# Up projections with the low and high part of x in one 512-column product, and the second layer's embedding product in four pieces elsewhere

## The chip, the cores and the metric

The kernel runs on one core of one Trainium2 chip. The metric is the device time of one execution in microseconds (us). A run's time is compared with runs of the kernel before; of the kernel before, three runs are given.

## The reference, cut to what matters

Two transformer blocks on one sequence of 256 tokens with 1024 features, all in float32. The first block has two layers. Each layer mixes tokens (layer 0 by two recurrences, layer 1 by attention), then has a feed-forward part and a gated embedding:

```
for l in range(2):
    x = x + mix(rms_norm(x, attn_norm[l]))
    h = rms_norm(x, mlp_norm[l])
    x = x + jnp.square(jax.nn.relu(h @ w_up[l])) @ w_down[l]      # 1024 -> 4096 -> 1024
    ple = rms_norm(p[l] @ ple_proj[l], ple_norm[l])               # 256 -> 1024
    x = x + ple * jax.nn.sigmoid(x @ ple_gate[l])
```

The second block follows with its own mixer and a mixture of 32 experts, of which all weights are read (some 200 MB).

## The kernel before, in words

Engines work through programs written out by hand, one per engine, each in order; they meet at semaphores. Weights come in units of 128 x 4096 floats (2 MB) through a ring of three slots; SP issues the loads in the order of a list of units, each when the unit three places earlier was read (L2836). The list of a layer's feed-forward part is: eight up units (512 of 4096 hidden features each), eight down units, one unit for the embedding's weights ("ple"), two gate units. Layer 1's ple stands between the last down unit and the gates.

Products of nearly full precision are made from rounded halves. A float32 weight w is split into high (w rounded to the matmul's short format, by ACT, `split_high` L2438) and low (w minus high, by DVE, `split_low` L1740, written over w in its ring slot); x likewise into `turned_high` and `turned_low` (ACT L2450, L2446; DVE L1755, L1750). A product then takes three passes, high x high, high x low and low x high (`three_passes`, L935), into the same columns of a PSUM bank. A unit is split in two halves; there are four buffers for high halves.

The up projection (`split_features`, `split_first`) holds weights still and streams x, 256 tokens: one half unit makes two blocks of 128 features, 256 columns each, in one bank of 512 columns. ACT evacuates a bank with ReLU (L2421) into one of four buffers `relu`; DVE squares it (L2077), rounds it (L2078) and takes the low part (L2079), which counts up `act_ready`. In each pass over a unit c, ACT first splits unit c + 1 (both halves), then evacuates the two banks of c; DVE does the same in its own order. The last pass splits the first down unit in place of an up unit.

`split_first` makes the first up unit in an order of its own, since the second half of x arrives late: half the features of two blocks, then a callback that turns the rest of x (transposes, L874), then what is left. Before the loop ACT also takes the norm's sums of squares and its square root (`norm`, L2426, L2427).

The down projection streams weights, 512 columns a product, 48 products a unit. After it x is turned again (`x_gate`), p is turned (L874), and for both layers the embedding product `p @ ple_proj` is made by `to_tokens` (L917: eight float32 products of 512 columns, two instructions each) while ACT and DVE make `turned_high` and `turned_low`; then come the gate products. POOL's queue loads p, the norms' rows and other small tables.

Attention's program for layer 1: six qkv units, transposes of q and k, the score and value products (`attend`), the output projection `w_o`. There are eight PSUM banks, taken in turn; PE waits before it takes one that was not read.

Of the kernel before, what the change touches and what calls it, by code (L numbers as in the profile page):

```python
# [7 lines left out]
P = 128  # L8
# [9 lines left out]
D = 1024  # L18
# [165 lines left out]
def weight_units(a):  # L184
# [55 lines left out]
def build(nc, a, out):  # L240
    ctx = ExitStack()
    with ctx:
# [140 lines left out]
        p_tok, pT = blocks(half(40), NT), blocks(half(41), 2)  # L383
        ple_raw, gate_s, ple_squares = (blocks(page(i, 2), NT) for i in (0, 2, 4))
# [125 lines left out]
        turned_high, turned_low = as_parts("turned_high", xn_at, KC * S), as_parts("turned_low", hT_at, KC * S)  # L510
# [358 lines left out]
        def _(pe):  # L869
# [67 lines left out]

            def split_features(name, tag, after=(None, None), first=False, turned_as=None):
# [28 lines left out]
            def split_first(name, tag, turned_as, between):  # L967

                pair = [banks.take(pe, *tag, s) for s in range(2)]

                def column(s, i, ks):
                    high, low_ = half_ready(name, s)
                    m = slice(i * P, (i + 1) * P)
                    for k in ks:
                        a = slice(k * S, (k + 1) * S)
                        if i == 0 and s == 0 and k % 2 == 0:
                            banks.wait_read(pe, *turned_as, k // 2)
                        last = three_passes(pair[s].ap[:, i * S:(i + 1) * S], high[:, k, m], low_[:, k, m],
                                            turned_high[:, a], turned_low[:, a], True, k == 0, k == KC - 1)
                    return last  # L980
# [6 lines left out]
                for s in range(2):  # L987
                    column(s, 1, range(KC)).then_inc(pair[s].full, 1)
                    half_read[(name, s)] = (pair[s].full, pair[s].use + 1)
                read_by(pair[1], *name)  # L990
# [382 lines left out]

            def feed_forward(l):
# [11 lines left out]
                split_first(("up", l, 0), ("up", l, 0), ("h_mlp", l), turn_late)  # L1386
                for c in range(1, 8):
                    split_features(("up", l, c), ("up", l, c))
# [9 lines left out]
                pe.wait_ge(sem("p_landed"), 16 * (l + 1))  # L1398
                bank = banks.take(pe, "pT", l)
                transposes([(bank.ap[:, k * S + t * P:k * S + (t + 1) * P], p_tok[:, t, k * P:(k + 1) * P])  # L1400
                            for k in range(2) for t in range(NT)], bank)
# [13 lines left out]
                banks.wait_read(pe, "pT", l)  # L1415
                w = blocks(weights(pe, "ple", l)[:, 0:2 * D], 2)
                for n in range(2):
                    bank = to_tokens(("ple", l, n), w[:, :, n * 512:(n + 1) * 512], pT, 2, 512)
                read_by(bank, "ple", l)
                def turn_early():  # L1420
                    pe.wait_ge(sem("ple_added"), NT)
                    turn_some(("h_att",), (0, 1))

# [40 lines left out]
            def turn_late():  # L1464
                pe.wait_ge(sem("ple_added"), 2 * NT)
                turn_some(("h_att",), (2, 3))

# [15 lines left out]
            turn_heads("kT", k_tok)  # L1483
            for tag in ("qT", "kT"):
                for c in range(4):
                    banks.wait_read(pe, tag, c)
            attend("att", lambda h: qT[:, h, :], lambda h: kT[:, h, :],
                   lambda h, k: v_att[:, k, h * P:(h + 1) * P], "att_prob", prob, probT)
            for c in range(4):
# [206 lines left out]
        def _(dve):  # L1696
# [366 lines left out]
            def feed_forward(l):  # L2063
                for c in range(8):
                    if c < 7:
                        split_low("up", l, c + 1)
                    else:
                        split_low("down", l, 0, 0)
                    if c == 0:
                        scales(2 if l == 0 else 4)  # L2070
                        step(v.tensor_tensor(rstd2, rstd, rstd, ALU.mult))
                    for i in range(2):
                        banks.wait_read(dve, "up", l, c, i)
                        buf = relu[:, (2 * c + i) % 4, :]
# [27 lines left out]
                for t in range(NT):  # L2102
                    step(v.scalar_tensor_tensor(ple_raw[:, t, :], ple_raw[:, t, :], ssq[:, t:t + 1], big_row,
                                                ALU.mult, ALU.mult))
                def add_gated(n):
                    for t in range(NT):
                        banks.wait_read(dve, "gate", l, n, t)
                        cols = slice(n * 512, (n + 1) * 512)
                        gated, part = ple_raw[:, t, cols], x3[:, t, cols]
# [91 lines left out]
            v.reciprocal(rstd, rstd).then_inc(sem("in2_scale"), 1)  # L2201
            dve.wait_ge(sem("in2_scale"), 1)
# [41 lines left out]
            v.reciprocal(cs, cs).then_inc(sem("latent_scale"), 1)  # L2244
            dve.wait_ge(sem("latent_scale"), 1)
# [90 lines left out]
            v.reciprocal(rstd, rstd).then_inc(sem("rstd_ready"), 1)  # L2336
            dve.wait_ge(sem("rstd_ready"), 1)
# [73 lines left out]
        def _(act):  # L2411
# [174 lines left out]

            def feed_forward(l):
                banks.read(act, "w_out" if l == 0 else "w_o", 0, 0)
                split_high("up", l, 0)
                take_highs(("h_mlp", l), range(KC // 2), lambda k: v1("mlp_norm", 8 * l + k))  # L2590
                for n in range(2):
# [17 lines left out]
                evacuate(pT, ACT.Copy, "pT", l)  # L2609
                take_highs(("x_gate", l), (2, 3))  # L2610
                for n in range(2):
                    for t in range(NT):
                        evacuate(ple_raw[:, t, n * 512:(n + 1) * 512], ACT.Copy, "ple", l, n, t)
# [4 lines left out]
                for t in range(NT):  # L2618
                    step(s.activation(ple_squares[:, t, :], ple_raw[:, t, :], ACT.Square, accum_out=ssq2[:, t:t + 1]))
# [20 lines left out]
                if l == 0:  # L2640
                    split_high("qkv", 0, halves=(1,))
                    take_highs(("h_att",), (0, 1), norm_weight)
                take_gate(1)
# [36 lines left out]
            norm(3, blocks(page(6, 2), NT))  # L2680
            for u, dst in enumerate((q_tok, q_tok, k_tok, k_tok, v_att, v_att)):
# [21 lines left out]
            for c in range(4):  # L2703
                evacuate(kT[:, 2 * c:2 * c + 2, :], ACT.Copy, "kT", c)
            attend("att", prob, probT, hT3)
# [3 lines left out]
            act.wait_ge(sem("in2_scale"), 1)  # L2709
# [308 lines left out]
```

## Time and profile before

| | us |
|---|---|
| median of three runs | 1401.24 (1400.96 to 1411.74) |
| span of the profiled execution | 1399.9 |
| busy: PE, DVE, ACT | 1186.8, 593.1, 436.0 |
| mean granted TensorE clock | 0.936 of 2.4 GHz |

The profile is of one execution. Its span runs from the first to the last instruction; the device time of the profiled execution is not given apart from it, and the runs' median is 1.3 us above the span. Busy times are unions of records; a record of a matmul covers its latency, and records of successive matmuls overlap. In the timeline's rows an "xN" merges N instructions of a kind, and brackets give the idle time before and what ended it.

### The profile page before, as it was taken

The page shows a single profiled execution, that of the slowest core. Times are in us where ns is not written, and L with a number is a line of the kernel's source. Part 1 is how long each engine was busy: PE and PEld are TensorE (multiplying, and loading weights), DVE is VectorE, ACT ScalarE, POOL GpSimd, SP SyncE. Part 2 cuts the span into 40 slices and gives each one's busy share as a digit, 9 for nine tenths or more (in the row PEclk, how much of TensorE's full clock was granted, in tenths as well). Part 3 has the DMA queues.
Part 4 walks back from the last instruction along what each step waited for, and adds up shares of the span by engine and source line. Part 5 has one row for each costly group of instructions (what it writes and reads, how often), then busy time and mean ns, then how long its engine had stood idle before and what let it go on. Part 6 is the DMA issues. An engine that isn't in the chain of part 4 may idle for free.

```text
span 1399.9 us, 19232 instructions
## 1 busy us (share of the span) xinstructions
PE 1186.8 (85%) x8218; PEld 868.8 (62%) x8218; DVE 593.1 (42%) x971; ACT 436.0 (31%) x689; POOL 22.6 (2%) x45
## 2 busy tenths in 40 slices
PE   6999989999999999999999999898664745647477
PEld 6998756699887787589988777654321312213132
DVE  5688413576643675366644548833100101001011
ACT  4653320344433585354433431543010000000001
POOL 4000000000000000000000000000000000000000
PEclk9999999999999999999999999999787868878699
DMA  8352669355554555145554624777999999999997
GB/s 274 132 205 97 211 214 360 128 181 181 189 207 174 204 180 180 61 162 185 185 190 151 228 88 152 270 297 299 426 427 430 427 428 428 429 427 431 427 422 281
DMA packets 103052, 362.98 MB, mean 259 GB/s; under 512 B 7844, under 2 KB 13296, under 8 KB 92096
## 3 DMA queue, kind: packets, MB, share of 16 engines
q1 hardware_dynamic: 100736, 357.64, 66.2%
q0 software_dynamic: 2096, 4.17, 1.1%
q8 instruction: 59, 0.97, 0.3%
q14 instruction: 17, 0.14, 0.0%
q10 hardware_dynamic: 144, 0.07, 0.0%
HBM read 360.81 MB, written 1.05 MB: 258 GB/s over the span
## 4 chain that ended last, share of the span: by engine, by line
PE 61%; DMA 22%; DVE 5%; issue 2%; ACT 2%; SPq 1%; DVEq 0%; ACTq 0%
PE bank L935 33%; DMA arena<-in_exp_w 20%; PE bank L637 8%; PE bank L1049 3%; PE bank L907 3%; PE bank L917 2%; PE bank L1242 2%; PE bank L874 2%; PE bank L1589 1%; DMA ring<-in_exp_w 1%; SPq L2843 1%; PE bank L1259 1%; PE bank L1273 1%; PE bank L1287 1%; PE bank L1456 1%
## 5 line engine op out<-in xcount | busy, mean ns | idle before, releaser
L637 PE MATMUL bank<-arena 128*32 128x512 f32 x880 | 187.2, 676 | 69.6 <-DMA arena<-in_exp_w 69.6
L1740 DVE TENSOR_TENSOR low_w<-ring,split_high 128x2048 fp32r<-128x2048 f32 x84 | 189.6, 2288 | 104.3 <-ACT split_high L2438 104.2
L935 PE MATMUL bank<-turned_high,low_w 128*128 128x256 f32 x720 | 204.6, 284 | 0.0
L2438 ACT ACTIVATE split_high<-ring 128x2048 fp32r<-128x2048 f32 x84 | 157.8, 1917 | 136.5 <-DMA ring<-in_w_down 67.7
L637 PE MATMUL bank<-ring,arena 128*32 128x512 f32 x528 | 98.1, 721 | 82.0 <-DMA arena<-in_exp_w 80.9
L935 PE MATMUL bank<-turned_high,split_high 128*128 128x256 f32 x512 | 145.9, 285 | 3.0 <-DVE turned_low L1755 3.0
L935 PE MATMUL bank<-turned_low,split_high 128*128 128x256 f32 x512 | 144.9, 283 | 0.0
L935 PEld LDWEIGHTS bank<-turned_high,low_w 128*128 128x128 f32 x720 | 139.1, 193 | 0.0
L637 PEld LDWEIGHTS bank<-arena 128*32 128x32 f32 x880 | 47.7, 123 | 128.8 <-issue 128.6
L789 DVE TENSOR_TENSOR arena<-arena,bank 128x512 f32<-128x512 f32 x8 | 5.5, 687 | 271.1 <-PE bank L637 243.2
L637 PEld LDWEIGHTS bank<-ring,arena 128*32 128x32 f32 x528 | 27.2, 129 | 148.5 <-issue 147.4
L2421 ACT ACTIVATE arena<-bank 128x512 f32<-128x512 f32 (+1 forms) x85 | 49.2, 594 | 165.2 <-PE bank L935 135.8
L935 PEld LDWEIGHTS bank<-turned_high,split_high 128*128 128x128 f32 x512 | 98.3, 192 | 3.9 <-issue 3.9
L935 PE MATMUL bank<-split_high,actT_high 128*128 128x512 f32 x256 | 99.6, 389 | 0.0
L935 PE MATMUL bank<-low_w,actT_high 128*128 128x512 f32 x256 | 99.6, 389 | 0.0
L935 PEld LDWEIGHTS bank<-turned_low,split_high 128*128 128x128 f32 x512 | 98.3, 192 | 0.5 <-issue 0.5
L838 ACT ACTIVATE arena<-bank 128x512 f32<-128x512 f32 x8 | 4.8, 597 | 238.9 <-PE bank L637 238.9
L935 PE MATMUL bank<-split_high,actT_low 128*128 128x512 f32 x192 | 74.7, 389 | 0.0
L935 PE MATMUL bank<-low_w,turned_high 128*128 128x512 f32 x176 | 68.6, 390 | 0.0
L935 PE MATMUL bank<-split_high,turned_high 128*128 128x512 f32 x160 | 63.3, 396 | 1.5 <-DVE turned_low L1755 1.5
L935 PE MATMUL bank<-turned_high,split_high_in 128*128 128x256 f32 x208 | 60.8, 292 | 3.1 <-DVE small L1792 3.1
L935 PE MATMUL bank<-split_high,turned_low 128*128 128x512 f32 x160 | 62.3, 389 | 0.0
(469 smaller groups left out, 1924.2 us busy)
## 6 DMA issues: line engine op xcount, KB each, us to landing
arena<-in_exp_w SPq DMA_DIRECT2D x51, 2048.0 KB, 23.6
ring<-in_exp_w SPq DMA_DIRECT2D x33, 2048.0 KB, 19.1
ring<-in_w_up SPq DMA_DIRECT2D x16, 2048.0 KB, 9.0
ring<-in_w_down SPq DMA_DIRECT2D x16, 2048.0 KB, 7.8
ring<-in_mod_w SPq DMA_DIRECT2D x12, 2048.0 KB, 8.5
arena<-in_exp_w SPq DMA_DIRECT2D x33, 512.0 KB, 13.8
ring<-in_w_in_ar SPq DMA_DIRECT2D x6, 2048.0 KB, 8.2
ring<-in_w_qkv SPq DMA_DIRECT2D x6, 2048.0 KB, 7.9
```

The costliest lines, as they stand in the source:

```text
L637: last = nc.tensor.matmul(mb[bank][strip(e), :], act[:, k, strip(e)], w[e][:, k, cols], start=(k == 0), stop=(k == n_k - 1), skip_group_ch ...
L874: last = nc.tensor.transpose(dst, src, ident[0:src.shape[0], 0:src.shape[0]])
L907: last = mm(bank.ap[:, i * S:(i + 1) * S], w[:, k, m:m + P], act[:, k, :], start=(k == 0), stop=(k == kcs - 1))
L917: last = mm(bank.ap[:, 0:n], act[:, k, t * P:(t + 1) * P], w[:, k, 0:n], start=(k == 0), stop=(k == kcs - 1))
L935: last = mm(dst, *pair, start=(start and i == 0), stop=(stop and i == 2))
L1049: last = mm(bank.ap[:, :], hT3[:, k, t * P:(t + 1) * P], w[:, k, :], start=(k == 0), stop=(k == KC - 1), skip_group_check=True)
L1242: last = mm(mod_bank.ap[strip, :], cond3[:, k, at:at + STRIP], w[:, k, :], start=(c == 0 and k < 4), stop=(c == MOD_UNITS - 1 and k >= 4), ...
L1259: last = mm(bank.ap[b, i * 64:(i + 1) * 64], near_invT[b, 4 * g + i, :], ident[b, b], start=True, stop=True)
L1273: last = mm(bank.ap[b, at], ab[b, 4 * g + i, 0, b], near_inv[b, 4 * g + i, :], start=True, stop=True)
L1740: v.tensor_tensor(low_of(name, s), half_of(slot(name), name, s), high_of(name, s).bitcast(F32), ALU.subtract).then_inc(sem("split_low"), 1)
L2421: s.activation(dst, src, func, scale=scale).then_inc(bank.freed, 1)
L2438: nc.scalar.activation(high_of(name, s), half_of(slot(name), name, s), ACT.Copy)\
```

## The change

The up projection: x low and x high now lie side by side in one tensor, `turned_parts`. For each block of 128 features and each k there is one product of 512 columns with the high weights (its first 256 columns come out as high x low, the others as high x high) and one of 256 columns with the low weights onto the second half of the bank. Each block of 128 features has a bank of its own. The two halves of the bank are added after the products: ACT copies the first half into `relu`, DVE adds the second. DVE then makes ReLU and square in one instruction, ACT rounds, DVE takes the low part one step later. The loops of ACT and DVE run in 16 steps of half a unit.

The embedding of layer 1: its unit leaves the ring; POOL's queue loads the weights into spare columns ahead of layer 0's feed-forward part, p is loaded and turned in the tail of layer 0, and four pieces of two products each are made in four places: in the first qkv unit, after the k transposes, after attention, and in `split_first` of layer 1. Buffers move accordingly, SP waits for `ple_added` ahead of four early expert loads that use the same columns, and a few semaphores are merged into one (`scales_ready`).

```diff
-        units.append((("ple", l), [(grid(0, 2, D), kcn(a["ple_proj"][l]))]))
+        if l == 0:
+            units.append((("ple", l), [(grid(0, 2, D), kcn(a["ple_proj"][l]))]))
...
+            def both_parts(bank, w_high, w_low, k):
+                low_and_high = blocks(turned_parts, 2)[:, :, k * S:(k + 1) * S]
+                high = turned_high[:, k * S:(k + 1) * S]
+                def by_high():
+                    return mm(blocks(bank.ap, 2), w_high, low_and_high, start=(k == 0), stop=(k == KC - 1),
+                              skip_group_check=True)
+                def by_low():
+                    return mm(bank.ap[:, S:2 * S], w_low, high, start=False, stop=False, skip_group_check=True)
+                if k == 0:
+                    by_high()
+                    return by_low()
+                by_low()
+                return by_high()
+            def split_up(name):
+                for s in range(2):
+                    high, low_ = half_ready(name, s)
+                    for i in range(2):
+                        m = slice(i * P, (i + 1) * P)
+                        bank = banks.take(pe, *name, 2 * s + i)
+                        for k in range(KC):
+                            last = both_parts(bank, high[:, k, m], low_[:, k, m], k)
+                        last.then_inc(bank.full, 1)
+                    half_read[(name, s)] = (bank.full, bank.use + 1)
+                read_by(bank, *name)
...
+            def late_ple(n, t):
+                bank = banks.take(pe, "ple", 1, n, t)
+                for k in range(2):
+                    last = mm(bank.ap[:, :], pT[1][:, k, t * P:(t + 1) * P], late_ple_w[:, k, n * 512:(n + 1) * 512],
+                              start=(k == 0), stop=(k == 1))
+                last.then_inc(bank.full, 1)
...
                 for c in range(1, 8):
-                    split_features(("up", l, c), ("up", l, c))
+                    split_up(("up", l, c))
```

The loop of DVE:

```diff
-                for c in range(8):
-                    if c < 7:
-                        split_low("up", l, c + 1)
-                    else:
-                        split_low("down", l, 0, 0)
-                    if c == 0:
+                def hidden_low(n):
+                    cols = slice(2 * n * S, 2 * (n + 1) * S)
+                    dve.wait_ge(sem("act_high"), 16 * l + n + 1)
+                    v.tensor_tensor(act_low(2 * n * S, 2 * S), relu[:, n % 4, :], actT_high[:, cols].bitcast(F32),
+                                    ALU.subtract).then_inc(sem("act_ready"), 1)
+                for n in range(16):
+                    c, i = n // 2, n % 2
+                    split_low(*(("up", l, c + 1) if c < 7 else ("down", l, 0, 0)), halves=(i,))
+                    if n == 0:
                         scales(2 if l == 0 else 4)
                         step(v.tensor_tensor(rstd2, rstd, rstd, ALU.mult))
-                    for i in range(2):
-                        banks.wait_read(dve, "up", l, c, i)
-                        buf = relu[:, (2 * c + i) % 4, :]
-                        chunk = 4 * c + 2 * i
-                        cols = slice(chunk * S, (chunk + 2) * S)
-                        step(v.tensor_tensor(buf, buf, buf, ALU.mult))
-                        step(v.tensor_copy(actT_high[:, cols], buf))
-                        v.tensor_tensor(act_low(chunk * S, 2 * S), buf, actT_high[:, cols].bitcast(F32), ALU.subtract)\
-                            .then_inc(sem("act_ready"), 1)
+                    else:
+                        hidden_low(n - 1)
+                    for m in (2 * i, 2 * i + 1):
+                        bank = banks.read(dve, "up", l, c, m)
+                        part = relu[:, n % 4, (m % 2) * S:(m % 2 + 1) * S]
+                        dve.wait_ge(sem("up_taken"), 32 * l + 4 * c + m + 1)
+                        v.tensor_tensor(part, part, bank.ap[:, S:2 * S], ALU.add).then_inc(bank.freed, 1)
+                        banks.wait_read(dve, "up", l, c, m)
+                    buf = relu[:, n % 4, :]
+                    v.scalar_tensor_tensor(buf, buf, 0.0, buf, ALU.max, ALU.mult).then_inc(sem("act_squared"), 1)
+                    dve.wait_ge(sem("act_squared"), 16 * l + n + 1)
+                hidden_low(15)
```

The loop of ACT:

```diff
-                for c in range(8):
-                    if c < 7:
-                        split_high("up", l, c + 1)
-                    else:
-                        split_high("down", l, 0, 0)
-                    for i in range(2):
-                        n = 2 * c + i
-                        if n >= 4 or l:
-                            act.wait_ge(sem("act_ready"), 16 * l + n - 3)
-                        evacuate(relu[:, n % 4, :], ACT.Relu, "up", l, c, i)
+                for n in range(16):
+                    c, i = n // 2, n % 2
+                    split_high(*(("up", l, c + 1) if c < 7 else ("down", l, 0, 0)), halves=(i,))
+                    if n >= 4 or l:
+                        act.wait_ge(sem("act_ready"), 16 * l + n - 3)
+                    for m in (2 * i, 2 * i + 1):
+                        bank = banks.read(act, "up", l, c, m)
+                        s.activation(relu[:, n % 4, (m % 2) * S:(m % 2 + 1) * S], bank.ap[:, 0:S], ACT.Copy)\
+                            .then_inc(sem("up_taken"), 1)
+                    act.wait_ge(sem("act_squared"), 16 * l + n + 1)
+                    s.activation(actT_high[:, 2 * n * S:2 * (n + 1) * S], relu[:, n % 4, :], ACT.Copy)\
+                        .then_inc(sem("act_high"), 1)
```

The queues of SP and POOL:

```diff
+            sp.wait_ge(sem("ple_added"), 4 * NT)
             load_early((1, 1), (1, 2), (1, 3), (2, 0))
...
             pool.wait_ge(sem("mixed_ready"), 1)
+            pool.dma_start(late_ple_w, kcn(a["ple_proj"][1])).then_inc(sem("p_landed"), 16)
```

## Rows read from the trace of the kernel before

**Rows 1.** The page's head.

```profile
span 1399.9 us, 19232 instructions
```

**Rows 2.** Chain of waits, layers 0 and 1 and gate: start us, us, what.

```profile
265.85 2.88 PE bank L935 x24
...
271.09 176.58 PE bank L935 x1128
...
604.27 165.72 PE bank L935 x1080
...
790.27 21.77 PE bank L935 x96
```

**Rows 3.** Busy us (count): PE, PEld, DVE, ACT, POOL; clock, DMA, GB/s.

```profile
271.00:360.00 89.00, 88.91 (x741) 88.94 (x742) 62.82 (x65) 40.06 (x36) 0.00 (x0) 1.00 0.49 174
553.00:570.00 17.00, 14.81 (x104) 12.39 (x104) 12.18 (x64) 14.62 (x53) 0.00 (x0) 1.00 0.25 92
960.00:1380.00 420.00, 261.32 (x1860) 107.06 (x1858) 38.46 (x110) 25.05 (x51) 0.00 (x0) 0.81 1.00 421
```

**Rows 4.** The page's costliest groups: line, engine, operation | busy us, mean ns.

```profile
L935 PE MATMUL bank<-turned_high,low_w 128*128 128x256 f32 x720 | 204.6, 284 | 0.0
```

**Rows 5.** Timeline, ACT then DVE, middle of layer 0's up projection.

```profile
303.10 0.60 ACT L2421 ACTIVATE arena<-bank 128x512 f32<-128x512 f32 x1 [5.16 <-PE bank L935]
303.59 3.71 ACT L2438 ACTIVATE split_high<-ring 128x2048 fp32r<-128x2048 f32 x2
...
303.73 0.69 DVE L2077 TENSOR_TENSOR arena<-arena 128x512 f32<-128x512 f32 x1 [3.49 <-ACT arena L2421]
...
304.91 0.69 DVE L2079 TENSOR_TENSOR actT_low<-arena,actT_high 128x512 fp32r<-128x512 f32 x1
305.54 4.50 DVE L1740 TENSOR_TENSOR low_w<-ring,split_high 128x2048 fp32r<-128x2048 f32 x2
309.95 0.68 DVE L2077 TENSOR_TENSOR arena<-arena 128x512 f32<-128x512 f32 x1
```

**Rows 6.** Groups by form, ACT, 272 to 363.

```profile
L2438 ACT ACTIVATE split_high<-ring 128x2048 fp32r<-128x2048 f32 x18 | 33.4, 1906 | 0.0
```

**Rows 7.** Timeline, DVE, operations like those that the change adds.

```profile
261.17 0.68 DVE L1735 TENSOR_TENSOR x<-x,bank 128x512 f32<-128x512 f32 x1
262.88 1.66 DVE L1755 SCALAR_TENSOR_TENSOR turned_low<-bank,vec,turned_high 128x256 fp32r<-128x256 f32 x4 [1.04 <-ACT turned_high L2450]
...
798.48 2.60 DVE L2103 SCALAR_TENSOR_TENSOR arena<-arena,small,big_row 128x1024 f32<-128x1024 f32 x2
```

**Rows 8.** Timeline, start of up: PE, ACT, DVE (layer 0), ACT (1).

```profile
271.09 0.36 PE L935 MATMUL bank<-turned_high,split_high 128*128 128x256 f32 x1 [1.50 <-DVE turned_low L1755]
...
273.22 3.70 ACT L2438 ACTIVATE split_high<-ring 128x2048 fp32r<-128x2048 f32 x2
...
279.94 0.69 DVE L2077 TENSOR_TENSOR arena<-arena 128x512 f32<-128x512 f32 x1
...
603.82 1.08 ACT L2426 ACTIVATE arena<-x 128x1024 f32<-128x1024 f32 x1
...
607.69 3.71 ACT L2438 ACTIVATE split_high<-ring 128x2048 fp32r<-128x2048 f32 x2
```

**Rows 9.** Timeline, end of layer 1: PE, DVE, SP's queue.

```profile
783.13 7.13 PE L917 MATMUL bank<-ring,arena 128*128 128x512 f32 x16
...
784.80 4.48 DVE L1740 TENSOR_TENSOR low_w<-ring,split_high 128x2048 fp32r<-128x2048 f32 x2
...
770.00 11.25 SPq L2836 DMA_DIRECT2D ring<-in_ple_gate  x2
```

**Rows 10.** Timeline around attention: PE, ACT, PE.

```profile
549.87 1.91 PE L874 MATMUL bank<-const,arena 128*128 128x128 f32 x16
...
552.72 1.28 ACT L2658 ACT_TABLE_LOAD   x1
...
570.46 2.81 PE L1049 MATMUL bank<-ring,hT 128*128 128x512 f32 x6 [0.99 <-ACT hT L2421]
```

More of the change, by code:

```diff
@@ L382, in build @@
         relu = blocks(page(8, 2), 4)
-        p_tok, pT = blocks(half(40), NT), blocks(half(41), 2)
-        ple_raw, gate_s, ple_squares = (blocks(page(i, 2), NT) for i in (0, 2, 4))
+        p_tok = blocks(half(40), NT)
+        pT = [blocks(half(41), 2), blocks(spare[:, 512:1024], 2)]
+        gate_s, ple_squares = (blocks(page(i, 2), NT) for i in (2, 4))
+        late_ple_w = blocks(spare[:, D:3 * D], 2)
+        ple_raw = [[page(0), page(1)], [spare[:, 3 * D:4 * D], const[:, const_first:const_first + D]]]
         cond3 = blocks(cond_strips[:, :], KC)
@@ L965, in split_features, with split_first @@
                         after[s]()
-            def split_first(name, tag, turned_as, between):
-                pair = [banks.take(pe, *tag, s) for s in range(2)]
+            def split_first(name, turned_as, between):
+                opened = {}
                 def column(s, i, ks):
@@ L973, in column @@
                     m = slice(i * P, (i + 1) * P)
+                    if ks[0] == 0:
+                        opened[(s, i)] = banks.take(pe, *name, 2 * s + i)
                     for k in ks:
-                        a = slice(k * S, (k + 1) * S)
                         if i == 0 and s == 0 and k % 2 == 0:
                             banks.wait_read(pe, *turned_as, k // 2)
-                        last = three_passes(pair[s].ap[:, i * S:(i + 1) * S], high[:, k, m], low_[:, k, m],
-                                            turned_high[:, a], turned_low[:, a], True, k == 0, k == KC - 1)
-                    return last
+                        last = both_parts(opened[(s, i)], high[:, k, m], low_[:, k, m], k)
+                    if ks[-1] == KC - 1:
+                        last.then_inc(opened[(s, i)].full, 1)
                 for s in range(2):
@@ L987, in split_first @@
                 for s in range(2):
-                    column(s, 1, range(KC)).then_inc(pair[s].full, 1)
-                    half_read[(name, s)] = (pair[s].full, pair[s].use + 1)
-                read_by(pair[1], *name)
+                    column(s, 1, range(KC))
+                    half_read[(name, s)] = (opened[(s, 1)].full, opened[(s, 1)].use + 1)
+                read_by(opened[(1, 1)], *name)
             def split_tokens(name, tag, after=(None, None), turned_as=None):
@@ L1372, in _, with turn_p @@
                 out_piece("w_out", n, t, range(4, KC))
+            def turn_p(l):
+                pe.wait_ge(sem("p_landed"), 32 * (l + 1) - 16 * l)
+                bank = banks.take(pe, "pT", l)
+                transposes([(bank.ap[:, k * S + t * P:k * S + (t + 1) * P], p_tok[:, t, k * P:(k + 1) * P])
+                            for k in range(2) for t in range(NT)], bank)
+            def late_ple(n, t):
[4 more added lines that the diff above has]
+                last.then_inc(bank.full, 1)
             def feed_forward(l):
@@ L1397, in feed_forward @@
                 turn_some(("x_gate", l), (0, 1))
[L1398 to L1401, printed above, removed]
+                if l == 0:
+                    turn_p(l)
                 for t in range(NT):
@@ L1413, in feed_forward @@
                     last.then_inc(bank.full, 1)
[L1415 to L1419, printed above, removed]
+                    banks.wait_read(pe, "pT", l)
+                    w = blocks(weights(pe, "ple", l)[:, 0:2 * D], 2)
+                    for n in range(2):
+                        bank = to_tokens(("ple", l, n), w[:, :, n * 512:(n + 1) * 512], pT[0], 2, 512)
+                    read_by(bank, "ple", l)
                 def turn_early():
@@ L2977, in _ @@
                 if l:
-                    pool.wait_ge(sem("ple_added"), 2 * NT)
+                    banks.read(pool, "pT", 0)
                 pool.dma_start(p_tok, a["p"][l, 0].rearrange("(t p) n -> p t n", p=P)).then_inc(sem("p_landed"), 16)
                 if l:
+                    pool.wait_ge(sem("ple_added"), 2 * NT)
                     pool.dma_start(big_row, a["ple_norm"][1].partition_broadcast(P)).then_inc(sem("big_row_landed"), 16)
```

56 lines of the change are left out of this document (38 added, 18 removed).

## The prediction

> **What bounds the kernel now.** I read the chain of waits first, to see who sets the end; then the stages' busy time and clock; then single instructions of the stages that the diff touches. The profiled execution spans 1399.9 us [rows 1]; the runs' median of 1401.24 lies 1.3 us above it, so I add to the span and keep that 1.3.
>
> In the chain the reader is to see that both feed-forward layers are one unbroken run of TensorE products: 1128 of them in 176.58 us from 271.09, 1080 in 165.72 us from 604.27 [rows 2]. In 271 to 360, the up projection of layer 0, PE is busy all 89 us at a granted clock of 1.00, the 2.4 GHz level, while DVE is busy 62.8 us and ACT 40.1 [rows 3]. So the up stage is TensorE's, and DVE and ACT follow it with room.
>
> The second thing to see is what one product costs. A record lasts 284 ns at 256 columns [rows 4], so leaving one out and making another 256 columns longer (0.107 at 2.4 GHz) looks like a gift of 0.177 us. But records overlap. By the chain, 24 products of 256 columns take 2.88 us, 0.120 each, and 96 of 512 columns take 21.77 us, 0.227 each [rows 2]. Only these spacings are time.
>
> **The up projection on PE.** Per block of 128 features and per k, three products of 256 columns (0.360 us) become one of 512 and one of 256 (0.347 us). That is 0.013 us saved, and 2 layers x 32 blocks x 8 k = 512 times 0.013 = 6.7 us in all. Half a unit (two blocks, 16 k) takes PE 5.55 us instead of 5.76.
>
> **The up projection on ACT and DVE.** Before, ACT rounds both halves of the next unit's weights and then evacuates two banks; DVE subtracts both, then squares, rounds and subtracts each hidden block. ACT never waits for that block's DVE work. In the new loop of 16 steps it does. Step n on ACT: round half a unit (split_high), copy the low parts of two banks, *wait until DVE has squared* (act_squared), round the square. On DVE: *wait for this step's split_high*, split_low, the low part of the hidden block before, two adds from PSUM, one max-and-square. Both queues run in order. So ACT's split_high of step n+1 stands behind its wait for DVE's square of step n, and DVE's split_low of n+1 stands behind that split_high: one ring through both engines. Its links:
>
> - split_high, 1.92 (two in 3.71 [rows 5], mean 1.91 [rows 6]) and 0.03 until DVE starts (303.10 + 0.60 to 303.73 [rows 5]);
> - split_low, 2.20 to the next DVE start (305.54 to 309.95 holds two, the second of which lasts 2.29 [rows 5]);
> - hidden low part, 0.63 (304.91 to 305.54 [rows 5]);
> - two adds of 256 columns from PSUM, each waiting for its own end. None stands in the trace. Four such scalar_tensor_tensors took 1.66, 0.41 each, and an add of 512 took 0.68 [rows 7]. I take 0.41 + 0.03, so 0.88; the bounds are 0.70 (half of 512's) and 1.40 (no cheaper than 512);
> - max-and-square of 512 columns, 0.70: between 0.65, half of the 1024-column form (two in 2.60 [rows 7]), and 0.75, the squaring's 0.68 [rows 5] with a little for the second operation;
> - 0.03, then ACT's rounding of 512 columns, 0.49 to the next ACT start (303.10 to 303.59 [rows 5]).
>
> The sum is c = 6.89 us a step, against 5.55 that PE needs for the half unit which a step prepares. ACT's two small copies run beside split_low, and the banks they read were filled long before, so they add nothing. With the low ends c is 6.66, with the high ends (and recorded lengths in place of start-to-start spacings) 7.72.
>
> Now the clock times, as if nothing ahead moved. Step 0's split_high starts at 273.22, after the norm; split_low and the scales follow (before, scales put 0.38 between split_low and the first square at 279.94 [rows 8]), so step 1 starts 6.64 later, at 279.86. Half unit n+2 is ready 4.24 (1.92 + 0.03 + 2.29) after step n starts. PE, resuming at 271.09, is through unit 0 near 279.4, unit 1's first half near 285.0, its second near 290.5. Step 2 delivers at 279.86 + 6.89 + 4.24 = 291.0: PE already waits, and from there on waits 1.34 a half unit. The ring carries on into the first down unit (steps 14 and 15) and into the split of the second, which starts one link after step 15, at 279.86 + 15 x 6.89 = 383.2, ready at 387.5. Before, PE began that down unit at 271.09 + 744 x 0.120 + 48 x 0.227 = 371.3. Layer 0 loses 16.2 us.
>
> Layer 1 is worse by its start: its norm loads a table, so split_high stands at 607.69 although PE resumed at 604.27 [rows 2, 8]. And the change puts a piece of the embedding product there: PE's transposes end some 1.5 us ahead of 604.27, as at 271.09 [rows 8], the piece ends near 604.5, ACT evacuates it in front of the norm (0.5), so the norm starts near 605.0 instead of 603.82 [rows 8]. Step 0 moves to 608.9, step 1 to 615.5; the second down unit is ready at 615.5 + 15 x 6.89 + 4.24 = 723.1, where 604.27 + 89.3 + 10.9 = 704.5 stood. Layer 1 loses 18.6 us. Together 34.8; each 0.1 us of c is worth 3 us (30 steps).
>
> After the second down unit nothing of this stays: a down unit takes PE 10.9 us and its splitting 4.5 on DVE.
>
> **The embedding product.** At the end of layer 1 the old place goes: 16 product instructions, 7.13 us from 783.13 [rows 9]; gate's run begins at 790.27 [rows 2]. What is late next is DVE. Gate's weights are in the ring two halves earlier (their load was issued at 770.00, when a ring slot came free [rows 9]; without the embedding's unit they take the slot before), so ACT no longer stands behind that load. But DVE's split_low of gate follows its four subtractions of the turned x, and these follow x itself; it started at 784.80 [rows 9] and starts some 0.4 earlier, 2.29 later gate may go: 786.7, and 0.3 for a first product after a wait. Gain 3.3 us, bounds 0 (DVE no earlier and held up) and 6.4.
>
> The four pieces cost PE 1.78 each (7.13 / 4) less the gap they fill. The first, in qkv's turn, lies in a gap ended by turned_low, as the one ahead of 271.09 (1.50 [rows 8]): +0.3. The second, after the kT transposes (from 549.87, 1.9 long), holds ACT's evacuation until 553.5 and so the table load that began at 552.72 [rows 10]: about +1.2, as attention starts with it. The third stands in the 0.99 gap at 570.46 [rows 10]: +0.8. The fourth is in the ring above. Four more transposes in layer 0: +0.4. Sum 2.7, bounds 0 (all in gaps) and 6, so part two comes to -0.6.
>
> POOL's queue takes a 1 MB load ahead of the layer-0 embedding's, over 170 us before either is read [rows 2], and the second p is loaded earlier; ACT and PE stand behind neither. SP's early expert loads get a wait for ple_added, over long before SP comes there: its queue has the ring's last loads ahead. Both cost nothing.
>
> The sum: 1399.9 + 34.8 - 0.6 = 1434.1 of span, and 1.3 around it: **1435.4 us**.
>
> **Rivals.** (A) Not slower: the ring does not close, because the queues let ACT's split_high pass the wait for DVE (a deeper run-ahead than the text shows). Place: every step; it decides at c = 5.55. For it: before, DVE's and ACT's busy sums leave room [rows 3], and even the new DVE sum of 4.4 a step is below 5.55. Against: both waits stand in program order, and nothing in the trace shows a later instruction of an engine passing a waiting one. Time: 1401.2 - 6.7 - 0.6 = 1394. The Trainium skill, Perfetto Trace Analysis, section Optimizing Tensor Performance (Matmuls), says that larger matmuls are more efficient where possible; by that rule this side would win. The trace agrees on PE's part (0.347 against 0.360) and shows how little it is.
>
> (B) The ring is there but shorter: ACT and DVE overlap a link, say hidden low (0.63) is off it and the adds are short: c = 6.1, 30 x 0.79 less: 34.8 - 23.7 = 11 on top: 1412. Against: DVE's program has the hidden low part ahead of the adds.
>
> (C) PE's new 1.3 us waits cost it its clock. Were the 24 halves after the first four of each layer at the 1.2 GHz level, a half would take about 16 x (0.44 + 0.227) = 10.7 instead of 6.89: 24 x 3.8 = 91 more, 1527. Against: attention, 553 to 570, full of waits for other engines, was granted 1.00; only the expert stage (960 to 1380), where PE was busy 261 of 420 us, was granted less, 0.81 [rows 3]. The Trainium skill, Perfetto Trace Analysis, section Matmul Optimizations, asks for matmuls back to back in batches, since the engine scales with use; no row here shows waits this short doing harm.
>
> (D) The records' lengths are the cost after all: 512 x 0.177 = 91 us less, 1310. The spacings exclude it.
>
> **How the numbers follow.** Forecast 0.80, A 0.06, B 0.10, C 0.03, D 0.01. With c from 6.5 to 7.5 the forecast reaches from 1424 to 1454. The range 1417 to 1454 leaves out about two in ten: A, C, D, half of B and the highest links. A measurement of this kernel tells about 1%, 14 us, from no change. Faster by over 1%: D and the far side of A, 0.03. Within 1%: most of A and half of B, 0.08. Slower: 0.89.
>
> **What would show it.** In the changed profile's up stages: PE idle some 1.3 us per half unit, released by DVE's split_low; split_high starting every 6.9 us, right behind an ACT rounding released by DVE; PE spacings of 0.227 and 0.120 in alternation at a clock of 1.00. At layer 1's end, gate starting about 6 us after the last down product instead of 9. Wrong it is if PE runs through the up stage without gaps, or if split_high starts more often than every 6.3 us.

## The result and the profile after

Six runs of the kernel after have a median of 1440.83 us (1438.57 to 1445.40), six of the kernel before in the same comparison 1402.84 (1400.96 to 1411.74). The ratio is 1.027, with a 95% interval of 1.0249 to 1.0292: slower by 38 us. The profiled execution took 1438.57 us with a span of 1436.8.

The first thing to read is the page's head, its section 4 and two groups of section 5, beside [rows 1] and [rows 4]. The share of PE in the chain is 47% (61% before), and ACT and DVE stand in it with their splits and squares.

```profile
span 1436.8 us, 18402 instructions
...
PE 47%; DMA 21%; DVE 11%; ACT 7%; issue 6%; SPq 1%; DVEq 0%; ACTq 0%
...
L950 PE MATMUL bank<-turned_parts,split_high 128*128 128x512 f32 x512 | 182.8, 403 | 27.0 <-DVE low_w L1798 25.0
...
L954 PE MATMUL bank<-turned_parts,low_w 128*128 128x256 f32 x512 | 132.7, 279 | 1.5 <-DVE turned_parts L1813 1.5
```

Of PE's groups on the page, the new 512-column product (L950) has by far the most idle time ahead of it that ACT or DVE ended: 25.0 us behind DVE's `split_low`, where the next group has 7.3. In [rows 3] the up stage of layer 0 had PE busy 88.91 of 89 us. In the kernel after it is busy 81.06 of 94, still at a granted clock of 1.00 (columns: busy of PE, PEld, DVE, ACT, POOL, then the clock, the DMA share and GB/s):

```profile
266.00:360.00 94.00, 81.06 (x450) 67.89 (x449) 57.02 (x69) 42.22 (x60) 0.00 (x0) 1.00 0.46 156
```

Next come two steps of the loop, first ACT's timeline, then DVE's and PE's, as the kernel before had them in [rows 5] and [rows 8].

```profile
298.00 0.63 ACT L2677 ACTIVATE actT_high<-arena 128x512 fp32r<-128x512 f32 x1 [4.00 <-DVE arena L2143]
298.54 1.90 ACT L2503 ACTIVATE split_high<-ring 128x2048 fp32r<-128x2048 f32 x1
300.35 0.63 ACT L2674 ACTIVATE arena<-bank 128x256 f32<-128x256 f32 x2
304.98 0.63 ACT L2677 ACTIVATE actT_high<-arena 128x512 fp32r<-128x512 f32 x1 [4.00 <-DVE arena L2143]
305.52 1.90 ACT L2503 ACTIVATE split_high<-ring 128x2048 fp32r<-128x2048 f32 x1
...
300.55 2.29 DVE L1798 TENSOR_TENSOR low_w<-ring,split_high 128x2048 fp32r<-128x2048 f32 x1 [2.57 <-ACT split_high L2503]
302.76 0.69 DVE L2125 TENSOR_TENSOR actT_low<-arena,actT_high 128x512 fp32r<-128x512 f32 x1
303.36 0.87 DVE L2140 TENSOR_TENSOR arena<-arena,bank 128x256 f32<-128x256 f32 x2
304.26 0.69 DVE L2143 SCALAR_TENSOR_TENSOR arena<-arena 128x512 f32<-128x512 f32 x1
307.53 2.29 DVE L1798 TENSOR_TENSOR low_w<-ring,split_high 128x2048 fp32r<-128x2048 f32 x1 [2.58 <-ACT split_high L2503]
...
309.87 0.50 PE L950 MATMUL bank<-turned_parts,split_high 128*128 128x512 f32 x1 [1.11 <-DVE low_w L1798]
```

One turn of the ring can be followed with a finger: ACT's `split_high` at 298.54, DVE's `split_low` behind it at 300.55 (after 2.57 us of idling for it), hidden low 302.76, adds 303.36, square 304.26, ACT's rounding at 304.98 (after 4.00 us of idling for DVE), and the next `split_high` at 305.52. That is 6.98 us a step, and each engine idles for the other once in it, so neither looks like a bound by its busy time. PE, which needs some 5.6, waits at the start of the half unit. Its row shows 1.11 us of idling and not the whole 1.38, since the last record ahead of the wait reaches past the spacing of its product and the first one behind it is longer (0.50 against 0.40).

The chain then shows when the second down unit begins (386.68 and 743.55), the first piece of the embedding (502.49) and how layer 1 ends. The transposes after layer 1's down projection (819.80) are a row of PE's timeline:

```profile
260.15 3.44 PE bank L1087 x8
...
386.68 76.42 PE bank L941 x336
463.09 2.18 PE bank L880 x20
...
502.49 1.72 PE bank L1423 x4
504.21 49.02 PE bank L941 x216
...
614.56 3.44 PE bank L1087 x8
...
743.55 76.42 PE bank L941 x336
...
819.80 2.12 PE L880 MATMUL bank<-const,x 128*128 128x128 f32 x16
...
821.07 2.48 DVE turned_parts L1808 x4
823.55 2.21 DVE low_w L1798
826.01 23.65 PE bank L941 x96
```

The chain and, for its last line, PE's timeline of the kernel before have these rows for the same marks, beside those of [rows 2]:

```profile
262.41 3.44 PE bank L1049 x8
...
488.13 49.25 PE bank L935 x216
...
595.60 3.43 PE bank L1049 x8
...
780.70 1.04 PE L874 MATMUL bank<-const,x 128*128 128x128 f32 x8
```

From mark to mark the two executions differ by this much, and this is what the prediction had for it:

| stretch | before | after | difference | predicted |
|---|---|---|---|---|
| mixer, to the last products of `w_out` | 262.41 | 260.15 | -2.3 | 0 |
| layer 0, to the transposes after down | 185.26 | 202.94 | +17.7 | +16.2 |
| its gate and the first piece, to the long qkv run | 40.46 | 41.12 | +0.7 | +0.7 |
| qkv and attention, to the last products of `w_o` | 107.47 | 110.35 | +2.9 | +2.0 |
| layer 1, to the transposes after down | 185.10 | 205.24 | +20.1 | +18.6 |
| from there to the gate products | 9.57 | 6.21 | -3.4 | -3.3 |
| gate products | 21.77 | 23.65 | +1.9 | 0 |
| what follows | 587.86 | 587.14 | -0.7 | 0 |
| span | 1399.9 | 1436.8 | +36.9 | +34.2 |

The first line is no part of the change. In the profiles of this study those products of `w_out` began between 260.15 and 264.30, and nothing ahead of them was edited. The last line moves as well: what follows the gate products, where only semaphores and one wait of SP's were edited, took between 586.9 and 590.3 us in these profiles, whether or not the kernel had that wait. So where two profiles are compared below, single stretches are compared, or the time from the last `w_out` products to the end of the gate products: 549.6 us before (262.41 to 812.04), 589.5 after (260.15 to 849.66).

### The profile page after: what moved, and what is told of

It reads as the page before. It is cut to its first block, busy times and chain, and to the rows that moved or that the text cites. A ratio compares the mean times of both kernels' runs of the same rounds, so it can differ in the third digit from the quotient of the medians.

```text
span 1436.8 us, 18402 instructions
## 1 busy us (share of the span) xinstructions
PE 1192.3 (83%) x7706; PEld 841.4 (59%) x7706; DVE 604.9 (42%) x1003; ACT 454.0 (32%) x753; POOL 23.3 (2%) x46
## 4 chain that ended last, share of the span: by engine, by line
PE 47%; DMA 21%; DVE 11%; ACT 7%; issue 6%; SPq 1%; DVEq 0%; ACTq 0%
DMA arena<-in_exp_w 20%; PE bank L941 19%; PE bank L643 7%; ACT split_high L2503 5%; PE bank L1087 3%; PE bank L913 3%; PE bank L880 2%; DVE arena L2140 2%; PE bank L1280 2%; DVE arena L2143 2%; PE bank L1647 1%; DVE low_w L1798 1%; PE bank L923 1%; ACT arena L2674 1%; DVE actT_low L2125 1%
## 5 line engine op out<-in xcount | busy, mean ns | idle before, releaser
L950 PE MATMUL bank<-turned_parts,split_high 128*128 128x512 f32 x512 | 182.8, 403 | 27.0 <-DVE low_w L1798 25.0
L954 PE MATMUL bank<-turned_parts,low_w 128*128 128x256 f32 x512 | 132.7, 279 | 1.5 <-DVE turned_parts L1813 1.5
L950 PEld LDWEIGHTS bank<-turned_parts,split_high 128*128 128x128 f32 x512 | 93.5, 188 | 52.9 <-DVE low_w L1798 33.1
L941 PE MATMUL bank<-split_high,turned_parts 128*128 128x512 f32 x320 | 100.6, 396 | 4.1 <-DVE low_w L1798 4.1
L954 PEld LDWEIGHTS bank<-turned_parts,low_w 128*128 128x128 f32 x512 | 96.5, 189 | 7.3 <-issue 2.8
L941 PE MATMUL bank<-turned_parts,split_high_in 128*128 128x256 f32 x416 | 77.9, 289 | 3.2 <-DVE small L1850 3.2
L941 PEld LDWEIGHTS bank<-split_high,turned_parts 128*128 128x128 f32 x320 | 60.5, 190 | 17.8 <-issue 5.3
L941 PE MATMUL bank<-low_w,turned_parts 128*128 128x512 f32 x176 | 69.1, 393 | 0.0
L941 PEld LDWEIGHTS bank<-turned_parts,split_high_in 128*128 128x128 f32 x416 | 66.4, 196 | 3.9 <-DVE low_w L1798 3.6
L2677 ACT ACTIVATE actT_high<-arena 128x512 fp32r<-128x512 f32 x32 | 20.2, 632 | 125.9 <-DVE arena L2143 125.9
L941 PE MATMUL bank<-turned_parts,low_w 128*128 128x256 f32 x208 | 59.6, 287 | 0.0
```

The lines of the kernel that those rows point to most:

```text
L941: last = mm(dst, *pair, start=(start and i == 0), stop=(stop and i == 2))
L950: return mm(blocks(bank.ap, 2), w_high, low_and_high, start=(k == 0), stop=(k == KC - 1), skip_group_check=True)
L954: return mm(bank.ap[:, S:2 * S], w_low, high, start=False, stop=False, skip_group_check=True)
```

## Experiments

### The two parts, each alone

The up projection's part alone keeps the embedding product in the ring and at the end of layer 1:

```diff
-        if l == 0:
-            units.append((("ple", l), [(grid(0, 2, D), kcn(a["ple_proj"][l]))]))
+        units.append((("ple", l), [(grid(0, 2, D), kcn(a["ple_proj"][l]))]))
...
-                    if l:
-                        late_ple(1, 1)
...
-            late_ple(0, 1)
...
-            late_ple(1, 0)
...
-            take_ple(1, 0, 1)
...
```

> Only the up projection's part of the change; the embedding of layer 1 stays in its old place. Ring theory (ACT's wait for the square and DVE's wait for split_high make one ring of 6.98 us a step): the loss stays, less the piece that stood ahead of layer 1's norm (1.2 us) and the embedding's own small sum: 1402.8 + 17.6 + 18.7 = 1439 us, c = 6.98. If the moved embedding product is what costs, this kernel is at 1402.8 - 6.7 = 1396 us.

Measured: 1440.74 us, ratio 1.0286 (1.0255 to 1.0317). The ring is whole: ACT's `split_high` starts at 301.37 and 308.35, 6.98 apart. Layer 0 takes 202.94 us, as in the kernel after, and layer 1, without a piece ahead of its norm, 204.04.

The embedding's part alone is the kernel before with those lines the other way:

```diff
+        if l == 0:
+            units.append((("ple", l), [(grid(0, 2, D), kcn(a["ple_proj"][l]))]))
...
+                    if l:
+                        late_ple(1, 1)
...
+                banks.wait_read(pe, "pT", 1)
+                late_ple(0, 0)
...
+            late_ple(0, 1)
...
+            late_ple(1, 0)
...
```

> Only the embedding's part; the up projection as before. Ring theory: within 0.3% of before. By the two profiles: -3.3 us at the gate, +3.1 around attention, +0.8 in layer 0's tail and qkv, and up to +1.8 since PE's clock falls after the longer wait ahead of the gate: 1403 to 1405 us. If the pieces carry the loss: 1430 us or more.

Measured: 1405.42 us, ratio 1.0018 (1.0001 to 1.0035). So the whole loss is the up projection's. The embedding's move, which saves 3.4 us at the end of layer 1, comes out at nothing or a loss of up to 5 us; by the stretches it loses 1.1 (550.7 against 549.6).

### One link out of the ring

```diff
-                    else:
-                        hidden_low(n - 1)
...
                     dve.wait_ge(sem("act_squared"), 16 * l + n + 1)
+                    if n:
+                        hidden_low(n - 1)
```

DVE's low part of the hidden block moves behind the square. The work is the same; only it no longer lies between ACT's `split_high` and the square for which ACT waits.

> The changed kernel with one DVE instruction of each step (the hidden block's low part, 0.61 us from start to start) moved from ahead of the adds to behind the square, where DVE waits for ACT anyway; the same work. Ring theory: the ring is shorter by that link, c = 6.98 - 0.61 = 6.37 us, and 30 steps give 18 us back: 1422 us. If the merged product or its banks set the pace, or DVE's total work does: no change, 1441 us.

Measured: 1422.46 us, ratio 1.015 (1.0124 to 1.0175). ACT's timeline shows the new step, with its wait for DVE down from 4.00 to 3.33, and DVE's has the adds right behind `split_low`:

```profile
303.58 0.63 ACT L2677 ACTIVATE actT_high<-arena 128x512 fp32r<-128x512 f32 x1 [3.33 <-DVE arena L2141]
304.12 1.90 ACT L2503 ACTIVATE split_high<-ring 128x2048 fp32r<-128x2048 f32 x1
...
310.42 1.90 ACT L2503 ACTIVATE split_high<-ring 128x2048 fp32r<-128x2048 f32 x1
...
306.05 2.29 DVE L1798 TENSOR_TENSOR low_w<-ring,split_high 128x2048 fp32r<-128x2048 f32 x1 [1.78 <-ACT split_high L2503]
308.25 0.87 DVE L2138 TENSOR_TENSOR arena<-arena,bank 128x256 f32<-128x256 f32 x2
```

6.30 us a step, 0.68 less: the link's 0.60 from start to start (302.76 to 303.36 above), and 0.08 by which DVE now starts sooner behind `split_high` (304.12 to 306.05 is 1.93, it was 2.01). Layer 0 takes 192.93 us instead of 202.94 and layer 1 195.26 instead of 205.24: 10.0 less in each, 0.67 in each of 15 steps. No engine's work had changed.

### The ring opened

```diff
+                def round_high(n):
+                    act.wait_ge(sem("act_squared"), 16 * l + n + 1)
+                    s.activation(actT_high[:, 2 * n * S:2 * (n + 1) * S], relu[:, n % 4, :], ACT.Copy)\
+                        .then_inc(sem("act_high"), 1)
...
                     split_high(*(("up", l, c + 1) if c < 7 else ("down", l, 0, 0)), halves=(i,))
+                    if n:
+                        round_high(n - 1)
...
-                    act.wait_ge(sem("act_squared"), 16 * l + n + 1)
-                    s.activation(actT_high[:, 2 * n * S:2 * (n + 1) * S], relu[:, n % 4, :], ACT.Copy)\
-                        .then_inc(sem("act_high"), 1)
+                round_high(15)
```

ACT rounds the square of step n behind `split_high` of step n + 1, so that its wait for DVE no longer holds up the split that DVE needs.

> The changed kernel with ACT's rounding of the square done one step later, behind the next split_high, so that ACT no longer waits in a step for that step's square; the same instructions. Ring theory: no ring is left, DVE's 4.4 us a step fits under PE's 5.6, PE runs through the up stage without gaps, and the time is before plus the embedding's part less 6.7 us: 1398 us (1394 to 1401). If the merged product or its banks set the pace: 1441 us.

Measured: 1399.18 us, ratio 0.9996 (0.9978 to 1.0014). ACT's timeline, then PE's:

```profile
300.65 1.91 ACT L2503 ACTIVATE split_high<-ring 128x2048 fp32r<-128x2048 f32 x1
302.46 0.62 ACT L2669 ACTIVATE actT_high<-arena 128x512 fp32r<-128x512 f32 x1
303.21 0.39 ACT L2681 ACTIVATE arena<-bank 128x256 f32<-128x256 f32 x1
305.96 0.39 ACT L2681 ACTIVATE arena<-bank 128x256 f32<-128x256 f32 x1 [2.37 <-PE bank L950]
306.25 1.91 ACT L2503 ACTIVATE split_high<-ring 128x2048 fp32r<-128x2048 f32 x1
...
306.23 0.40 PE L950 MATMUL bank<-turned_parts,split_high 128*128 128x512 f32 x1
306.46 0.28 PE L954 MATMUL bank<-turned_parts,low_w 128*128 128x256 f32 x1
306.58 0.39 PE L950 MATMUL bank<-turned_parts,split_high 128*128 128x512 f32 x1
```

ACT now idles for PE (L950) and not for DVE, and a step is 5.60 us. PE is the bound again; its pair of products takes 0.35 us (306.23 to 306.58), so a half unit 16 x 0.35 = 5.60. Layer 0 takes 182.64 us and layer 1 182.95, less than the 185.26 and 185.10 before. All that the ring had cost is back with two lines moved on one engine.

### What the wide product itself is worth

Taken apart into two products of 256 columns, once with the ring closed (the kernel after) and once with it open:

```diff
-                    return mm(blocks(bank.ap, 2), w_high, low_and_high, start=(k == 0), stop=(k == KC - 1),
+                    mm(bank.ap[:, 0:S], w_high, turned_low[:, k * S:(k + 1) * S], start=(k == 0), stop=(k == KC - 1),
+                       skip_group_check=True)
+                    return mm(bank.ap[:, S:2 * S], w_high, high, start=False, stop=(k == KC - 1),
                               skip_group_check=True)
```

> The kernel after, with the merged 512-column product taken apart into two of 256 columns (three products of 256 per k again; banks, engines' loops and buffers as in the kernel after). A half unit costs PE 16 x 3 x 0.120 = 5.76 us instead of 5.55. Theory (a ring through ACT and DVE sets a step of 6.98 us): PE's share is hidden, the time stays at that of the kernel after, 1441 within 3 us, split_high still every 6.98 us. Rival (PE sets the up stage in the kernel after too): 32 half units x 0.21 = 6.7 us more, 1447.5.

Measured with the ring closed: 1442.87 us, ratio 1.0287 (1.0267 to 1.0308), against 1.027 of the kernel after. The step is the same (ACT's rounding at 300.66 and 307.64, 6.98 apart), and so are the layers: 202.98 and 205.27 us against 202.94 and 205.24. In the kernel after, the product that the change is named for decides nothing.

> The kernel of e4_ring_open (ACT rounds a square one step later, behind the next split_high) with three products of 256 columns instead of one of 512 and one of 256. Theory: with the ring open PE sets the up stage, steps of 5.60 become 5.81 us, and the merged product is worth its 32 x 0.21 = 6.7 us: 1399.2 + 6.7 = 1406 (1404 to 1407.5). Rival (the merged product saves nothing even where PE binds, or ACT and DVE still set the step): within 2 us of e4_ring_open.

Measured with the ring open: 1404.77 us, ratio 1.0006 (0.9989 to 1.0022). Against the 0.9996 of the opened ring that is 1.4 us, give or take 3.4, so the times alone do not show what the wide product is worth; the rows do. ACT's steps are 5.76 (`split_high` at 299.44 and 305.20), as three products of 0.120 make them. Layer 0, from the last `w_out` products to the transposes after down, takes 185.26 us (264.30 to 449.56), exactly that of the kernel before; with the wide product it takes 182.64 (260.69 to 443.33). Layer 1 takes 185.34 and 182.95. So merging gains 2.6 and 2.4 us, 5.0 in all, where the expectation had 6.7.

### Versions that beat both

The up projection's part alone with the ring opened in the same way (the two edits shown above together):

> The up part alone with the ring open (ACT rounds a square one step later); the embedding product in its old place at layer 1's end. Theory (the two parts of the change add up, since each binds in its own stage): e4_ring_open less what the embedding's move cost alone (1405.4 less some 1402.4, 3 us): 1396 (1393 to 1398), gate products at a full clock, 21.8 us; 6.7 us below the kernel before but for what the two layers' ring start still costs. Rival (the old place at the end of layer 1 hides work that the open ring now needs, so that part of the 3.2 us of e4_ring_open is not regained): 1399 to 1401.

Measured: 1399.21 us, ratio 0.9966 (0.9950 to 0.9982); 1396 was missed, and the time lies in the range of the rival. The rows do not bear the rival out: the end of layer 1 takes 9.45 us (9.57 before), the gate products 21.79, and the layers 182.62 and 182.46. What was wrong is a size. The expectation took 3 us for the pieces from the times. By the ratios (0.9966 against 0.9996 with the pieces) they cost 4.2 us, give or take 3.4. By the stretches they cost 1.4, since the time from the last `w_out` products to the end of the gate products is 544.3 without them and 545.7 with them: 0.65 up to the long qkv run, 1.66 in qkv and attention, 0.49 in layer 1 and 1.84 in the gate products, less 3.24 ahead of the gate. Against the kernel before (549.6) this one gains 5.4.

Last, the opened ring with two pieces in the place that the profile of the kernel after offers, PE's wait ahead of layer 1's gate. ACT's evacuations of them move along, and its evacuation of the fourth piece moves from ahead of layer 1's norm to behind the first `split_high` of its loop:

```diff
+                if l:
+                    late_ple(0, 1)
+                    late_ple(1, 0)
...
-            late_ple(0, 1)
...
-            late_ple(1, 0)
...
-                if l:
-                    take_ple(1, 1, 1)
...
+                    if l and n == 0:
+                        take_ple(1, 1, 1)
...
```

> The kernel of e4_ring_open with two of the four embedding pieces (second half of the tokens of columns 0 to 511, and first half of columns 512 to 1023) moved out of attention, into PE's wait of 3.8 us ahead of layer 1's gate products, and ACT's evacuation of the fourth piece moved behind the first split_high of layer 1's up loop. Theory: attention gets back its 3.1 us; the pieces fill PE's wait (2 x 1.78 of 3.8), gate starts no later, and with PE busy there the gate products run at the clock of before (21.77 instead of 23.62 us): 1399.2 - 3.1 - 1.9 = 1394 (1392 to 1397). Rival 1 (the lower clock of the gate products does not come from PE's wait): 1396, gate products still 23.6 us. Rival 2 (ACT's two evacuations, 0.5 each, push back its high halves of x and so the gate): 1397 to 1399.

Measured: 1395.01 us, ratio 0.9947 (0.9926 to 0.9968), 7 us faster than before. PE's timeline ahead of the gate, and the gate's row of the chain:

```profile
777.61 3.60 PE L1423 MATMUL bank<-spare 128*128 128x512 f32 x8
...
781.87 0.70 PE L941 MATMUL bank<-split_high,turned_parts 128*128 128x512 f32 x2 [0.65 <-DVE low_w L1799]
...
781.87 22.04 PE bank L941 x96
```

Against the opened ring alone, qkv and attention take 107.24 us instead of 109.13, layer 1 182.45 instead of 182.95 and the gate products 22.04 instead of 23.63; they begin 6.21 us after the transposes, exactly as without the pieces. From the last `w_out` products to the end of the gate products that makes 541.7 us, 7.9 less than before. The two rivals are judged by those rows and not by the time, whose interval (1392.7 to 1398.6) holds the first and reaches into the second: the gate is not late, and its products are not at 23.6.

## Why the prediction was right, point by point

**The ring** was right as a mechanism. It stands in the timeline link by link, taking one link out of it shortened every step by that link and a little more (0.68 for 0.60), and moving one wait behind one split removed it. The step came out at 6.98 instead of 6.89 (the links as the prediction lists them add up to 6.88):

| link | predicted | measured |
|---|---|---|
| `split_high` to DVE's start | 1.95 | 2.01 |
| `split_low` to the next DVE start | 2.20 | 2.21 |
| hidden low | 0.63 | 0.60 |
| two adds | 0.88 | 0.90 |
| max-and-square to ACT's start | 0.73 | 0.72 |
| rounding to the next `split_high` | 0.49 | 0.54 |

The two operations that the trace of before did not show, the adds and the max-and-square, were sized within 0.02 from their nearest rows. The misses are in what [rows 5] did show: the 0.03 from ACT's end to DVE's start was 0.11 here (300.44 to 300.55), and the step from the rounding to the next ACT start 0.05 longer. 0.09 in each of 30 steps is 2.7 us, most of the 3.0 by which the two layers' losses (17.7 and 20.1) exceed the 34.8.

**The start of layer 1** went as said. Its piece of the embedding fills PE's gap ahead of 623.18, ACT's evacuation stands at 623.44 before the norm, and step 0's `split_high` at 627.77 is 4.59 us after PE resumes (623.18); the prediction had 608.9 - 604.27 = 4.6. It held that the piece delays this start by 1.2 us, and without the piece layer 1 takes 204.04 us instead of 205.24.

**The embedding's old place** gave 3.4 us where 3.3 was predicted, and by the named chain: four subtractions of the turned x from 821.07, `split_low` from 823.55, gate at 826.01. **Its four new places** cost 3.5 (0.66 and 2.88, the one in the ring apart) instead of 2.7. Of this, 1.2 belongs to this one execution: in its attention, from 573 to 578, the clock was granted at 0.66. The same stretch took 109.13 to 109.15 us, 1.2 less, in the five other kernels that have these pieces; in the one with three products and the ring closed the same products ran at 1.00 throughout. Without that the pieces cost 2.3 (41.13 and 109.13 us with the pieces alone, against 40.46 and 107.47).

**What failed** is a term that was not in the sum: "0.3 for a first product after a wait" was the whole price of having PE idle ahead of the gate. The gate's 96 products then took 23.65 us instead of 21.77, so of the 3.4 us won there 1.9 was paid at once. Rival C (a wait costs PE its clock) had been weighed for the up stage alone. There the trace went against it: 1.00 with a wait of 1.1 us in each half unit.

**The wide product** was priced at 0.347 us a pair by adding two spacings; alternating, it takes 0.35. This term lay under the ring, so the time did not show it. The Trainium skill, Perfetto Trace Analysis, section Optimizing Tensor Performance (Matmuls), holds larger matmuls to be more efficient; here, with PE as the bound, that came to 0.16 us of 5.76.

**The sum**: the span was 2.7 us above the forecast's 1434.1 (rings +3.0, pieces +0.8, gate products +1.9, old place -0.1, mixer and rest -3.0, rounding +0.1). That it came so close is partly luck: the mixer and what follows the gate products ran 3.0 us shorter in this execution, and hid that much of what the terms had missed. The median of the runs lay 4.0 above the profiled span where the kernel before had 1.3. Rival A (the ring does not close) fell with the first timeline, B (a step of 6.1) with the 6.98, D (records are the cost) with the opened ring, where 512 merged products gain 5.0 us and not 91.

## What to carry to other kernels

When two engines with queues in order hand work to each other twice in a loop, add up one turn of the handing, not their busy times: the turn is the step, even if both idle for half of it. Look for a wait that stands ahead of what the other engine needs next, and put the waiting instruction one step later; here that was worth about 40 us. Price an edit that shortens PE's work only after asking what the step is without PE, and look at what PE does in a gap before leaving it idle.

## What the runs showed of the hardware that was not expected

The clock after PE's wait ahead of the gate. The windows of the kernel after, around 826 (columns as above):

```profile
816.00:822.00 6.00, 5.90 (x34) 4.74 (x32) 2.44 (x4) 1.56 (x3) 1.07 (x2) 1.00 0.18 33
822.00:826.00 4.00, 0.00 (x0) 0.02 (x1) 4.00 (x5) 4.00 (x4) 0.00 (x0) 1.00 1.01 379
826.00:836.00 10.00, 9.99 (x37) 8.09 (x38) 9.00 (x6) 3.97 (x7) 0.00 (x0) 0.83 0.41 151
836.00:849.60 13.60, 13.60 (x63) 10.99 (x61) 4.15 (x6) 1.79 (x3) 0.00 (x0) 1.00 0.46 116
```

PE has nothing for 4 us, and of the 10 us that follow some are spent at the 1.2 GHz level (0.83 in the mean, 0.50 from 828 to 830), though PE is then busy without a gap. With eight product instructions of the embedding in that wait, and the DMA engines as busy (1.01), the same stretch was granted 1.00:

```profile
777.80:781.80 4.00, 3.41 (x8) 1.15 (x7) 4.00 (x5) 1.81 (x5) 0.00 (x0) 1.00 1.01 366
781.87:791.87 10.00, 10.00 (x44) 8.28 (x45) 9.78 (x8) 7.95 (x9) 0.00 (x0) 1.00 0.42 154
```

It repeats: the gate products took 23.41 to 23.65 us in the six profiled kernels in which PE waited there, 21.77 to 21.79 in the three with the whole embedding product ahead of them, and 22.04 with two pieces. The Trainium skill, Perfetto Trace Analysis, section Matmul Optimizations, asks for matmuls back to back; at this place the trace agrees, with 1.9 us, and in the up stage, with waits of 1.1 us, it shows no harm. Why the clock fell once in attention after a wait of 1.57 us, and not after the same wait in another execution, stays open.
